# A hybrid decoder layer on one core: the up projection by Strassen's scheme, and the down projection as a stage of its own

## What is computed

```python
x = x + rms_norm(merged @ w_o, g_post_mix)
up, ffn_state = causal_dwconv(rms_norm(x, g_pre_ffn) @ w_up, ffn_prev, w_conv_f, b_conv_f)
gate, val = jnp.split(up, 2, axis=-1)
x = x + rms_norm((jax.nn.gelu(gate) * val) @ w_down, g_post_ffn)
```

## Time and profile before

| | |
|---|---|
| three runs | 1764.22, 1764.5 and 1766.81 us, median 1764.5 |
| profiled execution | span 1762.5 us from first to last instruction |
| busy: PE, DVE, ACT, POOL | 1751.2, 1033.4, 593.0, 38.2 us |
| granted TensorE clock, mean | 0.999 of full speed |
| output projection on PE | 738.6 to 839.3 us |
| up and down projection on PE | 839.3 to 1629.4 us |
| moved by DMA | 137.06 MB |

### The profile page before, as it was taken

How to read it: one execution, slowest core, us unless ns; L and a number is a source line. 1 busy time by engine, 2 the same in 40 slices (tenths; PEclk the granted TensorE clock), 3 DMA queues, 4 the chain that set the end, 5 groups by cost and what they waited for, 6 DMA issues and landing times.

```text
span 1762.5 us, 28779 instructions
## 1 busy us (share of the span) xinstructions
PE 1751.2 (99%) x10306; PEld 1610.2 (91%) x10306; DVE 1033.4 (59%) x1900; ACT 593.0 (34%) x1048; POOL 38.2 (2%) x36
## 2 busy tenths in 40 slices
PE   9999999999999999999999999999999999999998
PEld 8988998998899899988999999999999999998886
DVE  6364155326415466566776666666667576668566
ACT  6444245344424552244311111111111111116665
POOL 1000000000000000000100000000000000003200
PEclk9999999999999999999999999999999999999999
DMA  5221221131232124443211111111111111114343
GB/s 181 86 64 63 86 78 50 58 98 56 68 88 64 52 101 149 167 147 114 69 50 38 48 49 48 37 45 51 50 37 49 37 48 49 36 57 180 112 138 114
DMA packets 159775, 137.06 MB, mean 78 GB/s; under 512 B 11807, under 2 KB 140155, under 8 KB 159676
## 3 DMA queue, kind: packets, MB, share of 16 engines
q1 hardware_dynamic: 148730, 130.89, 23.6%
q10 hardware_dynamic: 10946, 4.91, 1.0%
HBM read 108.57 MB, written 27.18 MB: 77 GB/s over the span
## 4 chain that ended last, share of the span: by engine, by line
PE 97%; DMA 1%; DVE 1%; ACT 0%; SPq 0%; issue 0%; DVEq 0%; ACTq 0%
PE pair L2117 11%; PE pair L2119 11%; PE pair L2118 11%; PE pair L2492 11%; PE pair L2188 10%; PE pair L2190 9%; PE pair L2189 9%; PE pair L2544 5%; PE pair L2543 5%; PE pair L2546 4%; PE pair L2142 4%; PE pair L2364 2%; PE pair L2334 2%; PE pair L2500 1%; DMA xn<-in_x_prompt 1%; PE pair L2590 0%
## 5 line engine op out<-in xcount | busy, mean ns | idle before, releaser
L2117 PE MATMUL pair<-bh,wh 128*128 128x384 f32 (+1 forms) x1008 | 330.6, 328 | 0.0
L2188 PE MATMUL pair<-xh,wh 128*128 128x384 f32 (+1 forms) x952 | 330.0, 347 | 0.0
L2119 PE MATMUL pair<-bh,wl 128*128 128x384 f32 (+1 forms) x1008 | 329.3, 327 | 0.0
L2118 PE MATMUL pair<-bl,wh 128*128 128x384 f32 (+1 forms) x1008 | 328.9, 326 | 0.0
L2190 PE MATMUL pair<-xh,wl 128*128 128x384 f32 (+1 forms) x952 | 311.9, 328 | 0.0
L2189 PE MATMUL pair<-xl,wh 128*128 128x384 f32 (+1 forms) x952 | 311.3, 327 | 0.0
L1464 DVE TENSOR_TENSOR wl<-raw,wh 128x1024 fp32r<-128x1024 f32 x112 | 137.0, 1223 | 125.9 <-ACT wh L882 125.1
L2188 PEld LDWEIGHTS pair<-xh,wh 128*128 128x128 f32 x952 | 179.1, 188 | 14.2 <-issue 11.5
L882 ACT ACTIVATE wh<-raw 128x1024 fp32r<-128x1024 f32 x112 | 118.5, 1058 | 213.7 <-PE pair L2544 96.8
L2117 PEld LDWEIGHTS pair<-bh,wh 128*128 128x128 f32 x1008 | 189.4, 188 | 0.8
L2118 PEld LDWEIGHTS pair<-bl,wh 128*128 128x128 f32 x1008 | 189.4, 188 | 0.4
(11 more groups left out here) (316 smaller groups left out, 2609.3 us busy)
## 6 DMA issues: line engine op xcount, KB each, us to landing
raw<-in_w_up SPq DMA_DIRECT2D x88, 256.0 KB, 3.2
raw<-in_w_in SPq DMA_DIRECT2D x80, 256.0 KB, 3.1
raw<-in_w_down SPq DMA_DIRECT2D x44, 256.0 KB, 2.7
gat<-gate_spill SPq DMA_DIRECT2D x16, 544.0 KB, 4.4
x_spill<-x SPq DMA_DIRECT2D x16, 512.0 KB, 2.9
gate_spill<-stg SPq DMA_DIRECT2D x32, 192.0 KB, 1.9
xn<-in_x_prompt SPq DMA_DIRECT2D x8, 512.0 KB, 8.0
pk<-in_cache_k SPq DMA_DIRECT2D x64, 64.0 KB, 1.8
```

Source lines behind the costliest of these rows:

```text
L2117: t_.matmul(b, h, xhi, start=(i == 0), stop=False)
L2118: t_.matmul(b, h, xlo, start=False, stop=False)
L2119: ins = t_.matmul(b, l, xhi, start=False, stop=(i == n - 1))
L2188: t_.matmul(b, h, xhi, start=(k == 0), stop=False, skip_group_check=True)
```

## The change

*Seven products for eight.* The 1024 prompt columns are cut into two halves of 512, the 1024 features of k into two halves of four blocks, and the pair of output blocks (gate, value) is the third cut: eight block products of 12 matmuls become seven, by the form of Strassen's scheme with shared sums. Three sums of the activations (sop, for products 6, 7 and 3) are made once, from hn: POOL forms them as rows (`s_rows`), PE turns them (six rounds of eight transposes, `round_`), ACT and DVE split them. Four sums of the weights (tb, tc) are made for every pair by POOL (`w_sums`), and split by ACT (`high_raw`) and DVE (`low_raw`). The results are combined out of PSUM: ACT copies product 1 to u2 and the sum of 1 and 2 to ug (`snapshot`, `c11`); DVE forms u2, u3 and the other three quarters.

*The samples* leave the tiles. `sample` multiplies the packed sample columns (high and low side by side) as the stationary operand by the weights, 16 matmuls of 256 columns; ACT copies the result, and two matmuls by a 0/1 matrix (`fold`) turn it back and add the parts.

*The convolution* runs over 1104 columns (prompt and padded samples in one), the first tap on ACT, the other two on DVE. The copies of the sums to ug and uv are gone from DVE; those of the conv states (fso) and pads move to POOL.

*Down projection.* The product of gate and value stays float32 and is written to DRAM (f_spill, 552 KB for a pair) by SP; once all 22 pairs are done, 11 chunks follow in a loop of their own, each reading two rows back into fraw, split by ACT and DVE. The transposes of p (`p_turned`), in the first pair before, stand between chunks 0 and 1. The first chunk copies to y where POOL set y to zero before.

*Order.* Block rows go through the output projection as 0, 4, 1, 5, 2, 6, 3, 7 and samples (ORDER), H_TURN has three other places, and the loads of w_up are four DMAs of 256 KB for a pair as before.

```diff
+ORDER = [0, 4, 1, 5, 2, 6, 3, 7, 8]
+HALF = SEQ // 2
+KH = KD // 2
+UPC = UW - 2
+NCH = NFF // 2
+UNITS = 2 * NBK
...
+            def s_rows(j):
+
+                ha, hb, (s2, s3, s4) = hn[0], hn[1], srow[j]
+                pool.wait_ge(d_h, 2 * j + 2)
+                if j == 3:
+                    pool.wait_ge(x1_out[1], 16 * 4)
+                then(minus(s3[:, :], ha[:, 0:HALF], hb[:, 0:HALF]))
+                g.tensor_tensor(hb[:, 0:HALF], hb[:, 0:HALF], hb[:, HALF:D], ALU.add).then_inc(g_s1, 1)
+                pool.wait_ge(g_s1, j + 1)
+                then(minus(s2[:, :], hb[:, 0:HALF], ha[:, 0:HALF]))
+                minus(s4[:, :], ha[:, HALF:D], s2[:, :]).then_inc(g_s, 1)
+
+            s_rows(0)
...
+            def w_sums(s, landed):
+
+                w = rawp[s]
+                pool.wait_ge(u_in[s], U_IN0 + landed)
+                minus(tc[:, 0, :, :], w[:, 1, 0:KH, :], w[:, 0, 0:KH, :]).then_inc(g_t, 1)
+                pool.wait_ge(g_t, i4.at(5))
+                minus(tb[:, 1, :, :], w[:, 1, KH:KD, :], tc[:, 0, :, :]).then_inc(g_t, 1)
+                minus(tb[:, 0, :, :], w[:, 1, KH:KD, :], w[:, 1, 0:KH, :]).then_inc(g_t, 1)
+                pool.wait_ge(g_t, i4.at(6))
+                minus(tc[:, 1, :, :], w[:, 0, KH:KD, :], tb[:, 1, :, :]).then_inc(g_t, 1)
...
+            def body(i, more=True):
+
+                states_out(i5.at(), 1)
+                if more:
+                    pool.wait_ge(d_ul, i4.at(3))
+                    w_sums((i + 1) % 2, i32.at(64 if i % 2 == 0 else 96))
+                pool.wait_ge(d_cv, i1.at())
+                pads(i)
...
+            def body(n, i, last=False):
+
+                s = (i - 1) % 2
+                act.wait_ge(p_q, i8.at())
+                high_raw(adh[:, 1, :, :], rawp[i % 2][:, 1, :, :])
+                tap_gate(s)
+                snapshot(i8.at(1), i5.at())
+                tap_val(s, i8.at(8 if i % 2 else 0))
+                gelu()
+                c11(i8.at(3))
+                sample_out(i8.at(4))
+                if not last:
+                    a_part(i8.at(4), (i + 1) % 2, i32.at(64 if i % 2 == 0 else 96))
+                    b_part(i8.at(5))
+                else:
+                    down_high(32, 0, i8.at(4))
+                sample_in()
+                if not last:
+                    act.wait_ge(d_cv, i1.at())
+                    rows_in(i1.at(2), (i + 1) % 2)
+                states(n - 1, i1.at(1))
+                if not last:
+                    c_part(i8.at(7))
...
+            def body(i, last=False):
+
+                s = (i - 1) % 2
+                c12(i8.at())
+                low_raw(i4.at(4), adl[:, 1, :, :], rawp[i % 2][:, 1, :, :], adh[:, 1, :, :])
+                conv_gate(s)
+                u2_sum(i8.at(2))
+                conv_val(s)
+                times(s)
+                if not last:
+                    low_raw(i4.at(5), adl[:, 0, :, :], rawp[(i + 1) % 2][:, 0, :, :], adh[:, 0, :, :])
+                else:
+                    down_low(0, 1)
+                u3_sum(i8.at(5))
+                if not last:
+                    low_raw(i4.at(6), tbl[:, :, :, :], tb[:, :, :, :], tbh[:, :, :, :])
+                c22(i8.at(6))
+                c21(i8.at(7))
+                if not last:
+                    low_raw(i4.at(7), tcl[:, :, :, :], tc[:, :, :, :], tch[:, :, :, :])
...
+            conv_gate(1)
+            down_low(1, 2)
+            down_unit(0, 0, 0, True)
+            conv_val(1)
+            for b in range(1, 4):
+                down_unit(b, b, 0, True)
+            times(1)
+            for b in range(4, NBK):
+                down_unit(b, b, 0, True)
+            for j in range(2):
+                f_low_in(1, j, j + 3)
+            for b in range(NBK):
+                if b == 2:
+                    down_low(0, 3)
...
-            H_TURN = {(3, 2): 0, (3, 7): 1, (4, 5): 2, (5, 3): 3, (6, 1): 4, (6, 7): 5, (7, 6): 6}
+            H_TURN = {(3, 2): 0, (4, 0): 1, (4, 5): 2, (5, 4): 3, (6, 1): 4, (7, 1): 5, (7, 6): 6}
...
+            W_OF = {"1": (adh, adl, 0, 0), "2": (adh, adl, 0, KH), "3": (adh, adl, 1, KH), "7": (tbh, tbl, 0, 0),
+                    "6": (tbh, tbl, 1, 0), "5": (tch, tcl, 0, 0), "4": (tch, tcl, 1, 0)}
+
+            def x_of(n, k):
+
+                if n in "673":
+                    return tuple(t[:, k, :] for t in sop["673".index(n)])
+                k0, cols = {"1": (0, slice(0, HALF)), "2": (KH, slice(0, HALF)), "5": (0, slice(HALF, SEQ)), "4": (KH, slice(HALF, SEQ))}[n]
+                return bh[:, k0 + k, cols], bl[:, k0 + k, cols]
+
+            def product(n):
+
+                hi, lo, h, k0 = W_OF[n]
+                o = q_bank[n]
+                for k in range(KH):
+                    x, xlow = x_of(n, k)
+                    w, wlow = hi[:, h, k0 + k, :], lo[:, h, k0 + k, :]
+                    t_.matmul(o, w, x, start=n in "1675" and k == 0, stop=False, skip_group_check=True)
+                    t_.matmul(o, w, xlow, start=False, stop=False, skip_group_check=True)
+                    ins = t_.matmul(o, wlow, x, start=False, stop=k == KH - 1, skip_group_check=True)
+                ins.then_inc(p_q, 1)
+
+            def sample():
+
+                for k in range(KD):
+                    for t in (adh, adl):
+                        ins = t_.matmul(s_bank, pack[:, k, :], t[:, :, k, :], start=k == 0 and t is adh, stop=k == KD - 1 and t is adl, skip_group_check=True)
+                ins.then_inc(p_q, 1)
+
+            i1, i4, i5, i96 = (Count() for _ in range(4))
...
+            pe.sem_inc(p_st, 1)
+            pe.wait_ge(d_ul, 1)
+            pe.wait_ge(d_nrm, BLK - 1)
+            pe.wait_ge(d_bl, 2 * (BLK - 1))
+            product("1")
+            for r in range(3):
+                round_(r)
+            pe.wait_ge(a_snap, 1)
+            product("2")
+            pe.wait_ge(d_rl, 6)
+            h_turn(BLK - 1)
+            for r in range(3, 6):
+                if r == 3:
+                    pe.wait_ge(d_bl, 2 * BLK)
+                round_(r)
+            pe.wait_ge(d_ul, 3)
+            pe.wait_ge(d_rl, 8)
+            product("6")
+            pe.wait_ge(d_rl, 10)
+            product("7")
+            pe.wait_ge(d_rl, 12)
+            pe.wait_ge(d_bl, 2 * BLK)
+            h_turn(BLK)
+            pe.wait_ge(d_fold, 1)
+            pe.wait_ge(d_bl, 2 * NBK)
+            sample()
+            pe.wait_ge(d_ul, 4)
+            product("5")
+            pe.wait_ge(g_foldm, 1)
+            fold()
+            pe.wait_ge(d_q, 2)
+            product("4")
+            rows_turned(192)
+            pe.wait_ge(d_q, 3)
+            product("3")
...
+            def body(last=False):
+
+                pe.wait_ge(d_ul, i4.at(1))
+                pe.wait_ge(a_c11, i1.at())
+                product("1")
+                pe.wait_ge(d_ul, i4.at(2))
+                product("6")
+                pe.wait_ge(a_snap, i1.at(1))
+                product("2")
+                pe.wait_ge(d_ul, i4.at(4))
+                pe.wait_ge(a_scp, i1.at())
+                sample()
+                pe.wait_ge(d_q, i5.at(-1))
+                product("7")
+                pe.wait_ge(a_smp, i1.at())
+                fold()
+                if not last:
+                    pe.wait_ge(a_rows, i1.at(1))
+                    rows_turned(i96.at(192))
+                pe.wait_ge(g_so, i1.at())
+                pe.wait_ge(a_st, i1.at())
+                pe.sem_inc(pe_held, 1)
+                states_turned()
+                pe.wait_ge(d_ul, i4.at(3))
+                pe.wait_ge(d_q, i5.at())
+                product("5")
+                pe.wait_ge(d_q, i5.at(2))
+                product("4")
+                pe.wait_ge(d_q, i5.at(3))
+                product("3")
...
```

1123 lines of the change are left out of this document (661 added, 462 removed).

## The result

| | before | after |
|---|---|---|
| median (4 runs each) | 1764.39 us | 1753.15 us (1751.5 to 1753.78) |
| ratio, 95% interval | | 0.9934, 0.992 to 0.9948 |
| profiled execution, span | 1762.5 us | 1751.3 us |
| granted TensorE clock, mean | 0.999 | 0.993 |
| FFN on PE | 790.1 us | 776.7 us (841.52 to 1618.17) |

The changed kernel is 11.2 us faster, 0.66%; 20.0 were forecast. The time is inside the range, and 1.4 us above the number of the clock's rival.

The account below looks back on a forecast made before the run. PE, busy 1751.2 of 1762.5 us, was taken as the bound. FFN terms 0.5 + 42.0 + 455.7 + 271.9 = 770.1 against 790.1 us, 20.0 less: span 1742.5, median 1744.5 us, range 1729 to 1767.

Parts of the forecast that it names:

- the clock's rival: First pair and chunk 0: clock falls in the two long waits; 7.2 us more, 1751.7 us; chance 0.12.
- The loop: Steady pairs: 21.7 us a pair instead of 23.82, so 455.7 us for 21 pairs (451.5 to 483).
- wait for u3: Each pair of the loop: PE waits 0 to 0.4 us for DVE's u3 before product 4; taken as 0.2.
- The fold: Samples in each pair: two matmuls of 64 columns, with two small transposes 0.5 us in all.
- Rival A: Loop: DVE with POOL becomes the bound, u3 late in every pair; 23.0 us a pair, 1771.8 us; chance 0.10.
- My upper bound: Loop: DVE and all of POOL one after the other, 15.1 + 6.2 + 1.7 = 23.0 us a pair.
- The first pair: Uncovered start of the FFN's pairs: 28.4 us of PE work plus waits, 42.0 us; bounds 34 and 50.
- the 2.4 for POOL's instructions: First pair: eight POOL instructions lying in DVE's way add 2.4 us.
- The down projection: Eleven chunks at 23.60 us, 259.6, plus waits and turns at the start: 271.9 us; bounds 265 and 284.
- the rows land some 8 us later: Chunk 0 of the down projection: chunk 1's rows land at 20.5, are split by 24; PE waits 5.0 us.
- the weights behind it in the queue: Start of the down projection: weights queued behind the rows read back cost 1.0 us.
- Rival C: Half clock after waits of 6.5 and 5.0 us, in first pair and chunk 0: 7.2 us more; chance 0.12.

Follow-up runs that it names:

- e7: Changed kernel with POOL making each of its four weight sums of a pair twice; 1769.76 us, one run.
- e1: Changed kernel with DVE's low parts of the second chunk's rows moved between the first chunk's last copies; 1749.19 us.
- e9: Changed kernel with second chunk's weights loaded before p and rows, last-stage loads later, ACT's high parts reordered to match, p turned between first-chunk units; 1743.92 us.
- e5: Changed kernel with 50 idle transposes on TensorE in the first pair's long wait, ahead of round 2; 1751.06 us.
- e6: Changed kernel with 56 idle transposes on TensorE in the long wait of the down projection's first chunk; 1752.38 us.
- e11: e9 plus e4's first-pair order, with block 7's hn also turned ahead of product 2 and split ahead of the samples' squares and scaling; 1740.62 us.
- e4: Changed kernel with ACT and DVE splitting rounds 0 and 1 ahead of the samples' work and a weight sum in the first pair; 1749.23 us.
- e3: e1 with p turned between first-chunk units, ACT's last-stage weights after p's high parts, and gain vectors loaded later; 1748.56 us.
- e12: e11 with most ACT and DVE splitting for the first pair's products put ahead of the samples' chain; 1741.06 us.

## Why the prediction was right, and where it was off

*The cause.* Right: PE was the bound, its list became shorter, and the loop of pairs brought the gain. 23.82 us a pair became 21.80, and 21 pairs with the way to the first chunk took 458.3 instead of 500.2, 41.9 less. The other stretches gave 28.4 back: first pair 41.9 against 23.8 (18.0 us), down projection 276.5 against 259.6 (16.9), less the 6.5 us of transposes and wait that stood in the old sum. That is 13.5 for the FFN (790.1 to 776.7). The output projection took 0.6 us more (0.5 forecast), and the chance loss of clock near the start 1.6; so 11.2.

*The loop*, forecast 21.7 us a pair and 455.7, measured 21.80 and 458.3, of which some 0.5 lie between the last pair and the first chunk. Two errors of opposite sign stand behind the small difference. No wait for u3 came (0.2 forecast; DVE's u3 ran from 897.88 to 898.56, and product 4 wanted it at 899.6). The fold is four matmuls, 0.48 us, where I had counted two, and with the two small transposes it takes 0.8 where I had 0.5. 512 columns at 0.227 and 256 at 0.12 held. Nine of DVE's fourteen instructions read two SBUF tiles, and not eight; the 11.7 us that I gave them are those of nine.

*Rival A* did not come, and e7 shows that its point is further off than I had it: with double POOL work the pair takes 22.54. My upper bound, DVE and all of POOL in a row, was 23.0 for one set. The DVE passes of 1.37 became 2.28 beside POOL, as laid out.

*The first pair*: 42.0 forecast, 41.9 measured. The single waits were 6.8, 1.6, 0.8 and 1.1 (forecast 6.5, 2.5, 1 and 1.2); the lower clock, 1.5 to 2.1 us there, is in it, and PE's own work took some 1 us more than the 28.4. Against that, 0.9 us of the waits and the 2.4 for POOL's instructions, which I had added to them, didn't come. So the size is partly luck.

*The down projection* is the mis-sized step: "the rows land some 8 us later, at 20.5; ACT and DVE split them by 24". The wait was 7.4 us and not 5.0, and 37.6 to 38.8 us went by to the second chunk where my terms make 33.9 (23.6 with 1.0, 5.0 and 4.3). The step left out ACT's list: a table load and three weights of the last stage stood ahead of the rows' high part. e1 took the wait away and got 2.6 to 3.7 of its 7.4 us. The next limit, which I had priced at 1.0 as "the weights behind it in the queue", was the order of p, rows and weights, on SyncE and on ACT; e9 changed both together. The old orders cost 7 to 10 us in all (276.5 to 279.2 against 269.1).

*Rival C, the clock*, had 0.12 beside the forecast, as if one excluded the other. It happened: the clock fell in both long waits, and PE worked at the lower level behind them. Its 7.2 us are too many. By the rows it is 1.5 to 2.1 in the first pair; in the down projection of the first profile seven intervals that average 0.45 instead of 0.227, 1.6, and eight of 0.43 behind the turns of p, 1.6, with 0.3 in the turns: 5.0 to 5.6 in all, part of which lies in the shadow of other waits. e5 gives 0.9 to 1.3 back for its 1.5 to 2.1, e6 nothing measurable. That the time nearly met the rival's number, 1751.7, is mostly a sum of other things: of the 8.8 us that the span lies above the forecast 2.6 are from the loop, 4.5 from the down projection with its clock and 1.6 chance. The Trainium skill ("TensorE: Matmul & The Clock Gate", What's actually happening) puts the idle array at 1.2 GHz and lets work bring it back to 2.4; the trace agrees, with 0.56 and 0.50 of full clock around the two waits. That a wait of 6.8 us can bring it down and so can a chain of short ones (e6) is shown by this case.

*What stays open*: e9 and e11 still have waits of 1 to 3 us in the first two chunks, and the way from the second chunk to the gate is 239.2 and 239.9 us in them where 236.0 and x2's turn (1.0) would do. The rows of e9 point to ACT's weights for the last stage; no run moved those alone. Nor was the order of the loads tried with ACT's order as it was.

## What to carry to other kernels

Where one engine is the bound and a change saves it a share of a steady loop, the forecast is settled by the places where the loop's cover is missing: the first round and the hand-over to the next stage took 28 of 42 us here. At such a hand-over, list for every engine and for the DMA queue what stands ahead of the thing that is wanted first, things for later stages included; moving those back on the queue and on ACT (e9, 9.4 us) was worth more than the order on DVE alone, the engine that seemed to hold (e1, 4.2 us). A removed wait must be followed to the next: e1 and e4 gained 30 to 50% of the length of the wait that they removed, e3 made a new one of 2.8 us by its own order on ACT, and two orderings of the same DVE work (e11, e12) came out the same.
